# 48 early expert chunks in place of 36, with one low part in four made by VectorE inside the top-16 search

## What is computed

```python
q = (tok @ w_q).reshape(n_tok, PEER_HEADS, 2, PEER_HALF)
s = einsum('nhpc,hpkc->nhpk', q, sub_keys)          # 8 heads, 2 halves, 128 keys
s_top, i_top = top_k(s, 16)
cand = s_top[:, :, 0, :, None] + s_top[:, :, 1, None, :]   # 16 x 16 per head
best, pos = top_k(cand, 16)
gate = softmax(best)                                # 128 experts of 16384 per token
act = gelu(einsum('tkd,td->tk', u_emb[expert], tok)) * gate
out = einsum('tk,tkd->td', act, v_emb[expert])
```

## Time and profile before

| what | value |
|---|---|
| median of three runs | 2329.22 us |
| the profiled execution | 2329.45 us |
| its span | 2327.7 us |
| TensorE matmul busy | 2237.0 us (96%) |
| VectorE busy | 1641.1 us (71%) |
| ScalarE busy | 1040.9 us (45%) |
| GpSimd busy | 110.3 us (5%) |
| mean DMA rate | 155 GB/s |
| one load of 512 KB, issue to landing (median) | 3.3 us |

### The profile page before, as it was taken

The page is one execution under the profiler, slowest core; times in us unless marked ns, Lnnn a source line. Parts: engine busy times, 40 slices in busy tenths (PEclk is TensorE's granted clock), DMA queues, the critical chain, the costliest instruction groups (busy, mean ns, idle before and its releaser), DMA issues. The chain is left out here.

```text
span 2327.7 us, 45798 instructions
## 1 busy us (share of the span) xinstructions
PE 2237.0 (96%) x18076; PEld 2103.1 (90%) x18076; DVE 1641.1 (71%) x3090; ACT 1040.9 (45%) x1693; POOL 110.3 (5%) x42
## 2 busy tenths in 40 slices
PE   7999999999999998999799998989999999999997
PEld 7999789999999787999789988989999998888886
DVE  5665768765765676875586577699889965777775
ACT  5444455444444355544353344344444444333333
POOL 0000000000000000000000000089000000000000
PEclk9999999999999999999899999999999999999999
DMA  5553535553555442556231225445444454555553
GB/s 189 176 195 133 172 110 163 175 198 126 181 180 185 139 146 100 163 183 208 92 126 66 99 80 178 137 145 172 145 140 142 138 169 165 191 192 193 189 191 134
DMA packets 99244, 361.09 MB, mean 155 GB/s; under 512 B 11496, under 2 KB 15224, under 8 KB 98944
## 3 DMA queue, kind: packets, MB, share of 16 engines
q1 hardware_dynamic: 99072, 358.64, 45.9%
HBM read 357.55 MB, written 1.05 MB: 154 GB/s over the span
## 5 line engine op out<-in xcount | busy, mean ns | idle before, releaser
L949 DVE TENSOR_TENSOR w_lo<-ring,w_hi 128x1024 fp32r<-128x1024 f32 (+1 forms) x304 | 396.7, 1307 | 225.6 <-ACT w_hi L750 224.9
L750 ACT ACTIVATE w_hi<-ring 128x1024 fp32r<-128x1024 f32 (+1 forms) x304 | 340.7, 1125 | 373.1 <-PE ps L448 342.7
L448 PE MATMUL ps<-x_hi,w_hi 128*128 128x272 f32 (+1 forms) x1568 | 454.3, 290 | 2.1 <-issue 1.0
L448 PE MATMUL ps<-x_hi,w_lo 128*128 128x272 f32 (+1 forms) x1568 | 451.1, 288 | 0.0
L448 PE MATMUL ps<-x_lo,w_hi 128*128 128x272 f32 (+1 forms) x1568 | 449.5, 287 | 0.0
L448 PEld LDWEIGHTS ps<-x_hi,w_hi 128*128 128x128 f32 x1568 | 295.3, 188 | 4.0 <-issue 1.9
L448 PEld LDWEIGHTS ps<-x_lo,w_hi 128*128 128x128 f32 x1568 | 295.4, 188 | 0.1
L448 PEld LDWEIGHTS ps<-x_hi,w_lo 128*128 128x128 f32 x1568 | 295.4, 188 | 0.0
L234 ACT ACTIVATE v_gated_hi<-ring 128x1024 fp32r<-128x1024 f32 x128 | 135.8, 1061 | 216.0 <-PE ps L2992 215.2
L2779 PE MATMUL ps<-tok_hi,u_mid_hi 128*128 128x256 f32 x736 | 213.6, 290 | 1.3 <-POOL u_mid_lo L240 1.3
L2779 PE MATMUL ps<-tok_hi,u_mid_lo 128*128 128x256 f32 x736 | 208.1, 283 | 0.0
(11 more groups left out here) (497 smaller groups left out, 5129.8 us busy)
## 6 DMA issues: line engine op xcount, KB each, us to landing
ring<-in_gate_up SPq DMA_DIRECT2D x176, 512.0 KB, 3.3
ring<-in_peer_v SPq DMA_DIRECT2D x128, 512.0 KB, 3.2
ring<-in_peer_u_mid SPq DMA_DIRECT2D x92, 512.0 KB, 3.3
ring<-in_down SPq DMA_DIRECT2D x64, 704.0 KB, 4.0
ring<-in_w_in SPq DMA_DIRECT2D x46, 512.0 KB, 3.3
ring<-in_peer_u_early SPq DMA_DIRECT2D x36, 512.0 KB, 3.3
ring<-in_project SPq DMA_DIRECT2D x32, 512.0 KB, 4.2
ring<-in_na_qk SPq DMA_DIRECT2D x16, 512.0 KB, 4.0
```

What stands on the lines that cost most here:

```text
L448: mm = nc.tensor.matmul(ps[:, bank, 0:ntok], parts[left][:, slot, t * P:(t + 1) * P], rhs[right][:, k, 0:ntok], start=start and n == 0, st ...
L750: A.activation(parts[0][:, n % SLOTS, 0:width[n]], ring[:, n % SLOTS, 0:width[n]], ACT.Copy).then_inc(hi_done.sem, 1)
L949: V.tensor_tensor(parts[1][:, n % SLOTS, 0:width[n]], ring[:, n % SLOTS, 0:width[n]], parts[0][:, n % SLOTS, 0:width[n]].bitcast(F32), ALU ...
```

## The change

`EARLY` is 48 and `MID` 80. The low parts of early chunks 0, 3, 7, 11, ... 47 (13 of 48) are made by VectorE, by calls of `low(i)` at fixed places of its search; GpSimd makes the other 35. Two semaphores count them, `pool_low` and `dve_low`, and all that waited for an early low part (SyncE's loads, TensorE) now waits for one of these. The low parts' buffer lies over `queries`, which are dead once the scores are made, so the first low part waits for both blocks of scores, and GpSimd waits for the first low part. After its last early low part GpSimd waits for VectorE's last one, adds 48 to `lo_done`, and goes on with the first two of the middle chunks. The core of the diff:

```diff
-EARLY = 36
+EARLY = 48
@@ peer
-            u_parts = [sb_in(c, f"u_early_{part}", [P, SLOTS, D], F32R) for part in ("hi", "lo")]
+            u_parts = [sb_in(c, "u_early_hi", [P, SLOTS, D], F32R),
+                       nc.alloc_sbuf_tensor_at("u_early_lo", [P, SLOTS, D], F32R, offset=gate_at + EARLY * SEQ * 4 + TOPK * 4)]
+        def wait_low(eng, slot, turn, back_by=0):
+            if slot == SLOTS - 1:
+                eng.wait_ge(dve_low.sem, turn + (1 - back_by))
+            else:
+                eng.wait_ge(pool_low.sem, turn * (SLOTS - 1) + (slot + 1 - back_by * (SLOTS - 1)))
@@ sync
-                load_stage(sp, "peer_u_early")
+                for i, slot, turn in grouped(sp, w.n, SLOTS):
+                    if early(i, SLOTS):
+                        continue
+                    wait_low(sp, slot, turn, back_by=1)
+                    load_item(sp, w, i, slot)
+                for i in range(SLOTS):
+                    wait_low(sp, i, EARLY // SLOTS, back_by=1)
+                    load_item(sp, wm, i, i)
+                sp.wait_ge(lo_done.sem, wm.first)
                 load_stage(sp, "peer_u_mid")
@@ tensor
-                pe_linear(pe, w, u_parts, x_parts, KD, SEQ, 4, bank0=4)
+                for i, slot, turn in grouped(pe, w.n, SLOTS):
+                    wait_low(pe, slot, turn)
+                    if not early(i, 4):
+                        pe.wait_ge(evac.sem, i + (evac.base - 3))
+                    for k in range(KD):
+                        for n, (left, right) in enumerate(TERMS):
+                            mm = nc.tensor.matmul(ps[:, 4 + slot, 0:SEQ], u_parts[left][:, slot, P * k:P * k + P], x_parts[right][:, k, :],
+                                                  start=(k == 0 and n == 0), stop=(k == KD - 1 and n == 2))
+                    mm.then_inc(mm_done.sem, 1)
@@ gpsimd
+                pool.wait_ge(pool_low.sem, 1)
                 for i, slot, _turn in grouped(pool, w.n, SLOTS):
-                    take_lo(pool, w, u_parts, i, slot)
+                    if slot == SLOTS - 1 or early(i, 1):
+                        continue
+                    pool.wait_ge(hi_done.sem, i + (w.first + 1))
+                    nc.gpsimd.tensor_tensor(u_parts[1][:, slot, :], ring[:, slot, 0:D], u_parts[0][:, slot, :].bitcast(F32), ALU.subtract).then_inc(pool_low.sem, 1)
+                pool.wait_ge(pool_low.sem, EARLY - EARLY // SLOTS)
+                pool.wait_ge(dve_low.sem, EARLY // SLOTS)
+                pool.sem_inc(lo_done.sem, EARLY)
@@ vector
+                def low(i):
+                    if i == 0:
+                        dve.wait_ge(scored.sem, 2)
+                    dve.wait_ge(hi_done.sem, i + (w.first + 1))
+                    slot = i % SLOTS
+                    V.tensor_tensor(u_parts[1][:, slot, :], ring[:, slot, 0:D], u_parts[0][:, slot, :].bitcast(F32), ALU.subtract).then_inc(dve_low.sem if i else pool_low.sem, 1)
@@ after the 16 maxima
+                        if tb == 0:
+                            low(7 if passes else 0)
@@ before n == 8 of the 16 positions
+                            if n == 8 and passes == 0:
+                                low(27 if tb else 3)
@@ after both passes
+                    if tb:
+                        low(31)
@@ after the 8 maxima of the candidates
+                        if tb or passes == 0:
+                            low((35, 39)[passes // 8] if tb else 11)
@@ after the 8 positions of the candidates
+                        if tb == 0 and passes == 0:
+                            low(15)
@@ after half_f
+                    if tb == 0:
+                        low(19)
@@ after the sum of half e
+                        if tb or e:
+                            low((43, 47)[e] if tb else 23)
```

More of the change, by code:

```diff
@@ L2687, in peer @@
     loaded, stored, v_step, mm_done, evac = (env[x] for x in ("loaded", "stored", "v_step", "mm_done", "evac"))
-    ring_full, load_stage = (env[x] for x in ("ring_full", "load_stage"))
+    ring_full, load_stage, load_item = (env[x] for x in ("ring_full", "load_stage", "load_item"))
     lo_done, hi_done = env["lo_done"], env["hi_done"]
@@ L2722, in peer @@
             total = sb_in(c, "peer_total", [P, 2, PH])
-            u_parts = [sb_in(c, f"u_early_{part}", [P, SLOTS, D], F32R) for part in ("hi", "lo")]
+            u_parts = [sb_in(c, "u_early_hi", [P, SLOTS, D], F32R),
+                       nc.alloc_sbuf_tensor_at("u_early_lo", [P, SLOTS, D], F32R, offset=gate_at + EARLY * SEQ * 4 + TOPK * 4)]
+            assert SLOTS * D == 2 * PH * SEQ
             scratch_end = nc.sbuf_base
@@ L2736, in peer @@
         w, wm = W["peer_u_early"], W["peer_u_mid"]
+        dve_low, pool_low = flags("dve_low", "pool_low")
         (scored, score_kept, picked, exp_in, exp_out, sel_turned, sel_copied, mid_done, mid_gelu, mid_taken, hots, spread,
```

## The result

The changed kernel takes 2335.28 us (median of seven runs, 2333.88 to 2340.12), the kernel before, measured beside it, 2329.22 us (2326.59 to 2330.91, seven runs). The forecast was 2331.8 us in a range of 2322 to 2337; the time lies in the range, 3.5 us above the forecast, and on the side, slower than 2333.9, that had a chance of 0.32.

The account below looks back on a forecast made before the run. TensorE, 96% busy, was taken as the bound, only its idle time changing. Start, chunks, stalls (7.2, 2.25, 2.8, 0.9) and 1.5 us exit put the transposes at 1672.4 against 1669.8 us: +2.6, so 2331.8 us, range 2322 to 2337.

Parts of the forecast that it names:

- TensorE bounds; only its idle time in the early stage counts.: Up to the transposes: TensorE busy 96%, matmuls unchanged, so only 10.8 us of early-stage losses can be won.
- The start.: Before chunk 0: TensorE starts at 1515.45 us, 1.2 us sooner, after 4.3 us idle; clock still falls.
- The turns carried over.: VectorE's wide operations and GpSimd's low parts alternate, about 2.1 us a wait; this cost was kept as before.
- the turns go away: Rival, chance 0.20: with GpSimd's smaller share VectorE and GpSimd no longer delay each other; gain 10.5 us, 2318.7 us.
- wide section: VectorE's wide two-input operations, two halves e per block; in block 0 counted at 20.1 us between chunks 19 and 23.
- 19 to 23: Between these chunks' low parts VectorE needs 21.3 us for 11.4; less the 2.6 window, TensorE stalls 7.2, clock 2.25 more.
- 39 to 43: Between these chunks' low parts in block 1: VectorE needs 16.8 us for 11.4, so TensorE stalls 2.8 us.
- every late low part waits for GpSimd: Rival, chance 0.27: VectorE's low parts at chunks 23, 43, 47 each lose 2.2 us to GpSimd; +9.2 us, 2338.4 us.
- 43 to 47, the exit.: End of early stage: stall 0.9 us before chunk 47, then TensorE stands 1.5 us before the transposes.
- The sum.: Time of the transposes: 1672.4 us against 1669.8 before, so +2.6 us, 2331.8 us against the median.
- more than one of the three: Deciding point: low parts delayed by GpSimd at more than one of chunks 23, 43, 47; +4.4 us, 2336.2 us.
- lower bound: Price of each low part on VectorE: 1.14 us, taken over 1.14 + 2.2 because GpSimd has pauses at most places.

Follow-up runs that it names:

- experiment 5: experiment 2 with places of chunks 3, 11 and 15 a little earlier and ScalarE making the first three high parts before waiting for scores: 2318.00 us.
- experiment 10: Kernel before, with only ScalarE making high parts 0 to 2 before it waits for the scores: 2329.87 us, ratio 1.0000.
- experiment 3: Changed kernel, its places kept, GpSimd subtracting only 128 of 1024 columns of each early low part (products not the reference's): 2319.3 us, one run.
- experiment 8: experiment 5 with ScalarE making the exponential before the last early gelu instead of behind it: 2318.83 us, ratio 0.9951.
- experiment 9: experiment 8 with 44 early chunks in place of 48: 2320.96 us, ratio 0.9961.
- experiment 1: Changed kernel with only chunk 23's low part moved, behind the first half of the wide section instead of both: 2335.07 us, ratio 1.0020.
- experiment 6: experiment 2 with VectorE's places for chunks 7 to 43 some 3 us later: 2337.16 us, ratio 1.0026.
- experiment 7: Changed kernel with 42 and 35 unread matmuls ahead of TensorE's waits for chunks 23 and 43: 2332.38 us, ratio 1.0012.
- experiment 2: Changed kernel with all places of VectorE's low parts moved so its work between them is as even as possible: 2320.34 us, ratio 0.9964.

## Why the prediction came out as it did

- *TensorE bounds; only its idle time in the early stage counts.* Right, and 10.8 us to be won was a good figure: from first chunk to transposes experiment 5 saves 153.3 - 144.5 = 8.8 us, some 2 of them by the clock of the first chunk. What the prediction did not say is that with 36 chunks none of it could be had (experiment 10).
- *The start.* Right: 1516.17 us in the trace, of which 0.6 is drift ahead of the stage, for 1515.45; idle 4.36 for 4.3; the clock fell. Experiment 5 took it away, for about 3 us that two overlapping intervals do not settle.
- *The turns carried over.* Right that they stay, and it decided the case: experiment 3 takes them away and gives 2319.3 us, for 2318.7 in the rival "the turns go away". But not all were carried over. The wide section of block 0 had three turns before, one in the earlier trace rows and these two, from VectorE's timeline in the kernel before; after, it has two (4.37 and 4.41).

```profile
1559.02 4.38 DVE L2902 TENSOR_TENSOR cand_rest<-half_f,iota_k 128x2048 f32<-128x2048 f32 x1
1563.43 4.36 DVE L2905 TENSOR_TENSOR cand_rest<-cand_rest,peer_idx_f 128x2048 f32<-128x2048 f32 x1
```

The Trainium skill ("SBUF — State Buffer", Who interferes with whom) has the shared port as a lock held for a whole instruction. The pairs above agree, with waits of 2.0 to 2.3 us.

- *19 to 23.* Right in place and nearly in size: 6.43 us for 7.2, at 1585 to 1591 us, clock at 0.50 behind it. In part this is luck: between the two low parts VectorE took the 21.3 us of the forecast, but the wide section was one turn shorter (18.1 us for 20.1) and the low part one turn longer (3.23 for 1.23). TensorE wanted chunk 23 0.7 us later than the forecast had it: chunk 19's low part was there about 3.0 us before TensorE came to it, for 2.6, and TensorE stood 0.27 us for GpSimd.
- *39 to 43.* **This is the term that was mis-sized**: 5.51 us for 2.8, and the clock fell behind it, which the sum left out. From the end of one low part to the end of the next it is 19.7 us for 16.8. Two things were missing. The low part itself waited 2.0 us for GpSimd, as in the rival "every late low part waits for GpSimd". And a small copy, 0.17 us in the kernel before, took 1.04: it ended as GpSimd's subtraction did.

The timeline of VectorE in the kernel after, in block 1, ahead of chunk 43's low part (as the earlier trace rows):

```profile
1640.70 1.04 DVE L2949 COPY peer_total<-best 128x8 f32<-128x8 f32 x1
...
1641.99 2.48 DVE L2953 TENSOR_SCALAR half<-pos 128x128 uint32<-128x128 uint32 x1
1644.38 0.21 DVE L2954 TENSOR_SCALAR half<-pos 128x128 uint32<-128x128 uint32 x1
...
1654.02 3.24 DVE L2902 TENSOR_TENSOR u_early_lo<-ring,u_early_hi 128x1024 fp32r<-128x1024 f32 x1
```

And that of GpSimd beside it:

```profile
1639.32 2.39 POOL L2836 TENSOR_TENSOR u_early_lo<-ring,u_early_hi 128x1024 fp32r<-128x1024 f32 x1 [3.52 <-ACT u_early_hi L234]
1641.96 2.42 POOL L2836 TENSOR_TENSOR u_early_lo<-ring,u_early_hi 128x1024 fp32r<-128x1024 f32 x1 [0.25 <-ACT u_early_hi L234]
```

The copy ends at 1641.74 us and GpSimd's first subtraction at 1641.71. The first of the two like operations behind it takes 2.48 us and the second 0.21; but it took 2.42 in the kernel before too, so the forecast, which carried the old intervals over, had that one. The Trainium skill ("SBUF — State Buffer", Who interferes with whom) lists copy, cast and `tensor_scalar` among the operations that can take the shared ports. The rows agree; the prediction had applied that section to two-input operations only.

- *43 to 47, the exit.* No stall before chunk 47 (0.9 forecast): VectorE waited 2.48 us for the high part, since TensorE had stood. The transposes waited 0.60 us for 1.5.
- *The sum.* From first chunk to transposes it said 1672.4 - 1515.45 = 157.0 us and 160.8 were measured. Term by term: chunk 43 + 2.7, its clock + 1.75 (gelu 5.0 us after the first matmul, for 3.25), two small waits (0.55 for ScalarE, 0.27 for GpSimd) + 0.8, chunk 23 - 0.8, chunk 47 - 0.9, exit - 0.9; that makes + 2.7, and the other 1.1 are spread over the stage.
- *The rivals.* Low parts behind GpSimd happened at two of the three places, 23 and 43: "more than one of the three", for which the text gave 2336.2 us and the measured time is 2335.3. So the rival with 0.27 was the truer description; that its time fits so well is in part luck, since at chunk 23 the turn that it adds was offset by the turn that the wide section lost. The reason given for the lower bound, that GpSimd has pauses at most places, holds at eleven of the thirteen places (1.22 or 1.23 us); it fails at the two where VectorE is late. GpSimd pauses only while it waits for the next high part (2.62 us at chunk 23, 3.52 at chunk 43), and a VectorE that comes late finds that pause over and GpSimd at the next two chunks. The prediction's sentence on the Trainium skill ("SBUF — State Buffer", Who interferes with whom), which added 3 x 2.2 us by the rule of that section, was nearer: two of the three came, with 2.0 us each.

## What to carry to other kernels

Work that is put by hand into another engine's program needs a table of windows: what the engine does between two places, waits for shared ports included, against what the consumer takes in that time. Being early at one place can't be saved up for the next, and even places were worth 15 us here, where the change as it stood lost 6. Before making something faster in a stage, ask what ends next: here the start alone and the number of early chunks alone gave nothing, more chunks with VectorE's help at uneven places lost 6 us, and all of it together with even places won 11 us (0.5%). And price an operation that can be held off by a busy neighbour at its upper bound wherever it is late already.

## What the runs showed of the hardware

- Who comes first matters at a tenth of a microsecond: VectorE's subtraction took 1.22 us where it started 0.05 us ahead of GpSimd's (experiment 5), and 3.37 and 3.36 us where it started 0.08 us behind (experiments 8 and 9). The Trainium skill ("SBUF — State Buffer", Who interferes with whom) says that the order of issue decides who blocks, not the shape of the operation; this is the case in small.
- A one-input operation of 128x8 elements can be held off as well: the copy above took 1.04 us for 0.17, and a 128x128 `tensor_scalar` 2.48 us where the next one like it took 0.21.
- A low clock came after idle times of TensorE of 2.46 us (experiment 8: 0.57 over the next 4 us), 2.64 us (experiment 1) and 2.71 us (experiment 6), not only after those of 4 to 6 us. It did not come after 1.97 us (experiment 5) or 1.92 us (experiment 9), nor after 1.61 and 1.55 us behind unread matmuls (experiment 7).
- The same idle time does not cost the same: after 4.36 us before chunk 0 the first matmul took 0.55 us in the changed kernel and in experiments 1 and 7, but 0.36 us in experiments 2, 3 and 6, where the clock fell only behind it. The gelu started 5.45 us after it in the changed kernel and 4.63 us in experiment 2.
- Keeping TensorE at work in two stalls with matmuls that nobody reads took 2.9 us off a median of 2335, without removing the stalls; the trace puts 3.7 us on the clock.
